# First expert's rows built by matmuls with a one-hot matrix, and each token's first expert row added by accumulating gathers at the end

## What is computed

```python
h2 = rms_norm(x, norm2_g[layer]) * (1 + sc2) + sh2
tokens = h2.reshape(b * n, d)
...
gates = jnp.sum(jax.nn.one_hot(idx, N_EXPERTS, dtype=F32) * wsel[..., None], axis=1)
for e in range(N_EXPERTS):
    he = jax.nn.silu(h @ w1[e]) * (h @ w3[e])
    y = y + gates[:, e:e + 1] * (he @ w2[e]).astype(F32)
...
x = x + g2 * f[:b * n].reshape(b, n, d)
return rms_norm(x, final_g)
```

## Time and profile before

| what | value |
|---|---|
| median of 3 runs | 601.15 us (600.04 to 601.83) |
| the profiled execution, its own time | 599.58 us |
| its span | 597.8 us |
| PE busy | 553.1 us (93%) |
| DVE busy | 442.8 us (74%) |
| ACT busy | 320.3 us (54%) |
| POOL busy | 155.7 us (26%) |
| HBM over the span | 294 GB/s |

### The profile page before, as it was taken

One profiled execution on the slowest core, in us unless ns is written; L12 is line 12 of the kernel. 1 busy time (PEld: TensorE's weight loads), 2 busy tenths in 40 slices (PEclk: granted clock), 3 DMA queues, 4 the chain that ended last, 5 costly groups with the idle time before them and its releaser, 6 DMA issues.

```text
span 597.8 us, 7516 instructions
## 1 busy us (share of the span) xinstructions
PE 553.1 (93%) x2681; PEld 412.6 (69%) x2681; DVE 442.8 (74%) x569; ACT 320.3 (54%) x394; POOL 155.7 (26%) x139
## 2 busy tenths in 40 slices
PE   1789998999999999985998999999999999999995
PEld 1345873677676787752577887888888888778772
DVE  1358693545586545428769999999999999999868
ACT  4530133345424922235438766768766768766624
POOL 5000916333220700023243113333112333110060
PEclk9789999999999999987999999999999999999998
DMA  8999997369223720058769999999999999999665
GB/s 309 389 371 321 379 369 254 101 191 357 72 70 128 247 84 36 35 210 303 241 227 390 365 398 391 392 392 392 389 392 391 390 392 390 370 383 369 209 213 210
DMA packets 89323, 172.05 MB, mean 288 GB/s; under 512 B 5514, under 2 KB 19022, under 8 KB 89298
## 3 DMA queue, kind: packets, MB, share of 16 engines
q1 hardware_dynamic: 83010, 153.34, 71.7%
q10 hardware_dynamic: 2768, 9.97, 4.1%
q0 software_dynamic: 3520, 8.42, 4.0%
HBM read 158.58 MB, written 17.32 MB: 294 GB/s over the span
## 4 chain that ended last, share of the span: by engine, by line
PE 76%; DMA 10%; DVE 5%; SPq 4%; ACT 3%; issue 1%; DVEq 0%; ACTq 0%; POOLq 0%
DMA ada<-in_ada_w 9%; PE psum L1209 5%; PE psum L1210 5%; PE psum L1211 5%; PE psum L1221 5%; PE psum L1220 5%; PE psum L1219 5%; PE psum L1236 4%; PE psum L1238 4%; PE psum L1237 4%; PE psum L934 3%; PE psum L936 3%; PE psum L935 3%; PE psum L1071 2%; PE psum L1183 2%; PE psum L1073 2%
## 5 line engine op out<-in xcount | busy, mean ns | idle before, releaser
L2116 DVE TENSOR_TENSOR w_lo<-w,w_hi 128x2048 fp32r<-128x2048 f32 x32 | 72.9, 2280 | 2.4 <-ACT w_hi L1622 2.4
L2105 DVE TENSOR_TENSOR w_lo<-w,w_hi 128x1024 fp32r<-128x1024 f32 (+2 forms) x30 | 68.7, 2293 | 0.0
L1622 ACT CAST w_hi<-w 128x2048 fp32r<-128x2048 f32 x32 | 60.3, 1918 | 10.7 <-DMA w<-in_moe_w 5.2
L1613 ACT CAST w_hi<-w 128x2048 fp32r<-128x2048 f32 x30 | 57.2, 1910 | 14.8 <-PE psum L1221 10.9
L2099 DVE TENSOR_TENSOR w_lo<-w,w_hi_a 128x2048 fp32r<-128x2048 f32 (+1 forms) x30 | 51.5, 1755 | 3.0 <-ACT w_hi_a L1609 2.7
L763 POOL COPY idx<-idx 128x1 int32 (+1 forms) x14 | 11.7, 833 | 153.0 <-PE psum L1183 152.4
L1236 PE MATMUL psum<-w_hi,heT_hi 128*128 128x512 f32 x120 | 49.7, 414 | 0.7 <-DVE w_lo L2116 0.7
L1238 PE MATMUL psum<-w_hi,heT_lo 128*128 128x512 f32 x120 | 47.0, 392 | 0.0
L1210 PE MATMUL psum<-w_lo,xgT_hi 128*128 128x512 f32 x120 | 46.8, 390 | 0.0
L1237 PE MATMUL psum<-w_lo,heT_hi 128*128 128x512 f32 x120 | 46.7, 389 | 0.0
L1219 PE MATMUL psum<-w_hi,xgT_hi 128*128 128x512 f32 x120 | 46.7, 389 | 0.0
(11 more groups left out here) (345 smaller groups left out, 1255.0 us busy)
## 6 DMA issues: line engine op xcount, KB each, us to landing
w<-in_moe_w SPq DMA_DIRECT2D x32, 2048.0 KB, 14.3
w<-in_moe_w SPq DMA_DIRECT2D x32, 1024.0 KB, 14.0
ada<-in_ada_w SPq DMA_DIRECT2D x12, 2048.0 KB, 18.1
win<-in_w_in SPq DMA_DIRECT2D x8, 1024.0 KB, 14.1
expert_rows<-ysb ACTq DMA_DIRECT2D x15, 512.0 KB, 6.3
expert_rows<-zero SPq DMA_DIRECT2D x1, 5120.0 KB, 21.3
wout<-in_w_out SPq DMA_DIRECT2D x4, 1024.0 KB, 4.9
x<-in_x SPq DMA_DIRECT2D x2, 1024.0 KB, 9.9
```

The lines of the kernel that those rows point to most:

```text
L1622: act.copy(w2_hi[:, :, hs], w2_sb[b][:, :, hs]).then_inc(w2_hi_ok[half], 1)
L2105: v.tensor_tensor(w3_lo[b][:, ks, :], w3_sb[b][:, ks, :], w3_hi[:, ks, :], ALU.subtract).then_inc(w3_lo_ok, n)
L2116: v.tensor_tensor(w2_lo[b][:, :, hs], w2_sb[b][:, :, hs], w2_hi[:, :, hs], ALU.subtract).then_inc(w2_lo_ok[half], 1)
```

## The change

The first expert's rows are no longer gathered. DVE compares slot numbers with the rank of expert 0 and multiplies by the token's choice and its norm factor (`hot_0`), PE multiplies `x1` with it, tile by tile (`first_rows`, eight feature chunks of four matmuls each), and ACT applies the norm's scale and shift of the feature (`norm_cols`) on the way to `xgT_0`. That buffer moves to the place of `xg[0]`, so that POOL clears and first uses `xg[0]` only after `plain3`. The two `keep_busy(WARM)` go, and the one ahead of the ranks gives three matmuls. At the end POOL adds each token's first row directly to `x1` by an accumulating indirect DMA; `add_first` and half of `gathered_row` go, and ACT's copy of tile 3 comes after the first tile's square.

```diff
@@ -153,6 +152,9 @@
         sq = at("sq", 196 * K1, [P, 512])
+        norm_cols = at("norm_cols", 195.125 * K1, [P, 2 * KD])
+        first_rank = at("first_rank", 195.625 * K1, [P, NT])
+        first_scale = at("first_scale", 195.75 * K1, [P, NT])
         rwq = at("rwq", 198 * K1, [P, KD, QC])
@@ -163,7 +165,8 @@
         ysb = [at(f"ysb_{b}", (176 + 4 * b) * K1, [P, D]) for b in range(2)]
-        xgT_0 = at("xgT_0", 180 * K1, [P, KD, P])
+        xgT_0 = at("xgT_0", 160 * K1, [P, KD, P])
+        hot_0 = at("hot_0", 184 * K1, [P, NT, P])
         hot_mod = at("hot_mod", 176 * K1, [P, NT * 2, P])
@@ -576,7 +579,7 @@
             load_first_w2(0)
-            sp.wait_ge(xg_in[0], 16)
+            sp.wait_ge(xg_in[1], 16)
             load_first(moe_w3, w3_sb, 1, w3_in)
@@ -746,7 +749,6 @@
             gp.wait_ge(logit_ok, NT + 1)
-            gp.memset(xg[0][:], 0.0)
             link(gp.memset(xg[1][:], 0.0))
@@ -765,8 +767,7 @@
-            for b in range(2):
-                gather_rows(b, idx[:, b:b + 1])
+            gather_rows(1, idx[:, 1:2])
@@ -784,6 +785,9 @@
             n_pairs = gp.value_load(ints[0:1, 8:9], min_val=0, max_val=OVER // 2) + NE // 2
+            gp.wait_ge(h3_ok, 1)
+            gp.sem_inc(gather_go, 1)
+            link(gp.memset(xg[0][:], 0.0))
             for b in range(2):
@@ -802,10 +806,12 @@
             for t in range(NT):
-                for k in range(2):
-                    gp.indirect_dma_start(ygat[:, t, k, :], None, y_dram,
-                                          bass.IndirectOffsetOnAxis(ap=slot_idx[:, t, k:k + 1], axis=0)
-                                          ).then_inc(gat_in[t], 16)
+                gp.indirect_dma_start(x1[:, t, :], None, y_dram,
+                                      bass.IndirectOffsetOnAxis(ap=slot_idx[:, t, 0:1], axis=0),
+                                      compute_op=ALU.add).then_inc(gat_in[t], 16)
+                gp.indirect_dma_start(ygat[:, t, 1, :], None, y_dram,
+                                      bass.IndirectOffsetOnAxis(ap=slot_idx[:, t, 1:2], axis=0)
+                                      ).then_inc(gat_in[t], 16)
@@ -1141,7 +1147,7 @@
-            keep_busy(1)
+            keep_busy(3)
             pe.wait_ge(prob_ok, 1)
@@ -1153,6 +1159,19 @@
+            def first_rows(k):
+
+                if k >= 4:
+                    pe.wait_ge(x0_ok, k - 3)
+                for t in range(NT):
+                    m = pe.matmul(bank[(0, 1, 4, 5)[k % 4]][:, 0:P], x1[:, t, k * P:(k + 1) * P], hot_0[:, t, :],
+                                  start=(t == 0), stop=(t == NT - 1))
+                m.then_inc(x0_ps, 1)
+
+            pe.wait_ge(rows_act, 8)
+            pe.wait_ge(hot0_ok, 1)
+            for k in range(4):
+                first_rows(k)
             pe.wait_ge(hot_ok, 1)
@@ -1168,26 +1187,23 @@
-            keep_busy(WARM)
-            pe.wait_ge(w1_lo_ok, 2)
-            keep_busy(WARM)
-            pe.wait_ge(rows_act, 8)
+            for k in range(4, KD):
+                first_rows(k)
...
-                pe.wait_ge(xg_in[b], i * 16 + 16)
-                if not (isinstance(s, int) and s == 0):
-                    pe.wait_ge(x_lo_ok, s)
+                pe.wait_ge(xg_in[b], (i + b) * 16)
+                pe.wait_ge(x_lo_ok, s)
                 for k in range(KD):
...
-                pe.wait_ge(x_lo_ok, 1)
                 pe.wait_ge(w1_in[0], 16)
                 for k in range(KD):
+                    pe.wait_ge(x0_ok, k + 1)
                     m = pe.matmul(bank[2][:], xgT_0[:, k, :], w1_sb[0][:, k, :], start=(k == 0), stop=(k == KD - 1))
@@ -1262,7 +1278,6 @@
-            rows_in(0, 0, 0)
             plain1()
@@ -1335,20 +1350,17 @@
             last_to_tokens(0, 1).then_inc(tok_ok, 1)
-            pe.wait_ge(x3_ok, 1)
-            for half in range(2):
-                last_to_tokens(3, half)
             pe.wait_ge(xsum_ok, 2)
...
             last_to_tokens(1, 1).then_inc(tok_ok, 1)
-            pe.wait_ge(gat_in[3], 32)
-            for half in range(2):
-                gathered_row(half, 0)
             pe.wait_ge(xsum_ok, 3)
...
             last_to_tokens(2, 1).then_inc(tok_ok, 1)
-            gathered_row(0, 1)
-            gathered_row(1, 1).then_inc(tok_ok, 1)
+            pe.wait_ge(last_act_ok, 3)
+            for half in range(2):
+                last_to_tokens(3, half)
+            gathered_row(0)
+            gathered_row(1).then_inc(tok_ok, 1)
@@ -1661,11 +1673,15 @@
             high_w1(1, 1, 0)
+            act.wait_ge(rwq_ok, 1)
+            for k in range(KD):
+                act.wait_ge(x0_ps, k + 1)
+                act.activation(xgT_0[:, k, :], bank[(0, 1, 4, 5)[k % 4]][:, 0:P], ACT.Identity,
+                               scale=norm_cols[:, k:k + 1], bias=norm_cols[:, KD + k:KD + k + 1]).then_inc(x0_ok, 1)
+            act.sem_inc(x_lo_ok, 1)
+            act.sem_inc(xt_ok, 1)
             high_w2(0, 0, 0, 0)
             high_w2(0, 0, 0, 1)
-            act.wait_ge(xt_ok, 1)
-            act.copy(xgT_0[:].rearrange("p k t -> p (k t)"), psum[:, 0:2, :].rearrange("p a n -> p (a n)")
-                     ).then_inc(x_lo_ok, 1)
             gate_half(0)
@@ -1700,17 +1716,19 @@
                 act.wait_ge((y0_copied, y1_copied)[half], last + 1)
-                act.copy(y_hi[:, hs], ysb[1][:, hs]).then_inc(ylast_hi_ok, 1)
-            act.wait_ge(fresh_ok, 4)
-            act.copy(psum[:, 6:8, :].rearrange("p a n -> p (a n)"), x1[:, 3, :]).then_inc(x3_ok, 1)
+                act.copy(y_hi[:, hs], ysb[1][:, hs]).then_inc(last_act_ok, 1)
...
                 act.activation(ygat[:, t, 0, :], psum[:, 2 * t:2 * t + 2, :].rearrange("p a n -> p (a n)"), ACT.Square,
-                               accum_out=st2[:, t, 6:7]).then_inc(ss3_ok, 1)
-                act.wait_ge(ss3_ok, t + 1)
+                               accum_out=st2[:, t, 6:7]).then_inc(ss2_ok, 1)
+                act.wait_ge(ss2_ok, 2 * NT + t + 1)
                 act.activation(st2[:, t, 7:8], st2[:, t, 6:7], ACT.Sqrt, bias=eps[:], scale=1.0 / D
-                               ).then_inc(root3_ok, 1)
+                               ).then_inc(root2_ok, 1)
+                if t == 0:
+                    act.wait_ge(gat_in[3], 32)
+                    act.wait_ge(fresh_ok, 4)
+                    act.copy(psum[:, 6:8, :].rearrange("p a n -> p (a n)"), x1[:, 3, :]).then_inc(last_act_ok, 1)
@@ -1959,6 +1977,7 @@
                 link(v.tensor_tensor(rwq[:], rw[:], bank[7][:, 128:136].unsqueeze(2).to_broadcast([P, KD, QC]), ALU.mult))
+                v.tensor_copy(norm_cols[:], bank[7][:, 128:144])
                 v.tensor_copy(shc[:], bank[7][:, 136:144].unsqueeze(2).to_broadcast([P, KD, 2])).then_inc(rwq_ok, 1)
@@ -2035,6 +2054,13 @@
             v.wait_ge(rank_ok, 1)
+            v.wait_ge(sel_ok, 1)
+            v.tensor_tensor(first_scale[:], sel[:, :, 0], st2[:, :, 4], ALU.mult)
+            link(v.tensor_copy(first_rank[:], bank[7][:, 0:NT * NE].rearrange("p (t e) -> p t e", e=NE)[:, :, 0]))
+            for t in range(NT):
+                ins = v.tensor_scalar(hot_0[:, t, :], iota_slot[:], first_rank[:, t:t + 1], first_scale[:, t:t + 1],
+                                      ALU.is_equal, ALU.mult)
+            ins.then_inc(hot0_ok, 1)
             pick(rank[:], bank[7][:, 0:NT * NE].rearrange("p (t e) -> p t e", e=NE).unsqueeze(2).to_broadcast(E2))
@@ -2202,22 +2228,19 @@
-            def add_first(t):
+            def add_second(t):
                 v.wait_ge(gat_in[t], 32)
-                link(v.tensor_tensor(x1[:, t, :], ygat[:, t, 0, :], x1[:, t, :], ALU.add))
-
-            def add_second(t):
                 v.wait_ge(fresh_ok, t + 1)
...
                 hs = slice(half * 512, (half + 1) * 512)
-                v.wait_ge(ylast_hi_ok, half + 1)
+                v.wait_ge(last_act_ok, half + 1)
                 v.tensor_tensor(y_lo[:, hs], ysb[1][:, hs], y_hi[:, hs], ALU.subtract).then_inc(ylast_lo_ok, 1)
...
             def result(t):
-                v.wait_ge(root3_ok, t + 1)
+                v.wait_ge(root2_ok, NT + t + 1)
                 link(v.reciprocal(st2[:, t, 5:6], st2[:, t, 7:8]))
@@ -2243,14 +2266,12 @@
             low_hidden(1, last)
-            add_first(0)
             expert_rows(1, last, final, 0)
...
             for t in (1, 2):
-                add_first(t)
                 add_second(t)
```

More of the change, by code:

```diff
@@ L67 @@
 K1 = 1024
-WARM = 2
 NC = N // 2 + 1
@@ L397, in build @@
         x_lo_ok = sem("x_lo_ok")
+        x0_ok = sem("x0_ok")
+        x0_ps = sem("x0_ps")
+        hot0_ok = sem("hot0_ok")
         w1_hi_ok = sem("w1_hi_ok")
@@ L411, in build @@
         xsum_ok = sem("xsum_ok")
-        x3_ok = sem("x3_ok")
         fresh_ok = sem("fresh_ok")
-        ylast_hi_ok = sem("ylast_hi_ok")
+        last_act_ok = sem("last_act_ok")
         ylast_lo_ok = sem("ylast_lo_ok")
         tok_ok = sem("tok_ok")
-        ss3_ok = sem("ss3_ok")
-        root3_ok = sem("root3_ok")
```

(6 more changed lines are left out.)

## The result

The changed kernel is slower: 605.56 us median (603.12 to 607.28) against 601.58 (600.04 to 604.01) of the kernel before, ratio 1.007 [1.0055 to 1.0084]. The forecast was 600.3; rival 2 (605.4, or 602.9 with rival 1's start) comes nearest. The profiled execution has a span of 603.4 us, 5.6 more than before, where the medians differ by 4.0: the profiled execution of the kernel before (599.58) is faster than each of its twelve timed ones (600.04 the lowest).

What follows compares the result with a forecast made beforehand. It took PE to bound the blocks, which keep their length; start +1.1 and end -1.95 gave -0.85 us on the median of 601.15, so 600.3, range 597.7 to 605.5 (the forecast's own 599 to 602).

Steps and rivals of the forecast that it cites:

- rival 2: End, ACT's wait ahead of tile 3's copy: accumulating gathers take twice as long, end +3.1, total 605.4; chance 0.32.
- rival 1: Start: the full clock holds from the first rows on, start -1.4, together -3.35, total 597.8; chance 0.25.
- both bounds: End, DMA engines' time per accumulating gather: at least a plain one's 1.48 us, at most 2.96.
- the slack I gave it: End, ACT's wait for tile 3's gathers: 0.85 us of later landing was taken to cost nothing.
- 5.9 - 0.85: End, accumulating gathers twice as long: 5.9 us more transfer time, less 0.85 of slack ahead of ACT's copy.
- the saving by the three additions and the round of `gathered_row`: End, DVE's additions and PE's gathered rows: last square starts at 590.3 instead of 592.25, -1.95 us.
- the same two changes of clock: Start: PE's clock falls at 273.7 and rises at 280.5, so index sums end at 281.9, 5.15 us later.
- the second term: Start, DVE's list behind the index sums: it can start 4.05 us later before PE's first output is late.
- The two gaps: Start, DVE's waits for PE in that list: 3.01 us ahead of 294.76 and 1.04 ahead of 302.53.
- the forecast's number: Start: index sums 5.15 later less 4.05 from DVE's gaps leave PE's first output +1.1 us.

Runs made afterwards that it cites:

- e5: The changed kernel with 25 spare matmuls on PE behind the records of tiles 0, 1 and 2 at the end; 603.67 us, ratio 1.0045 to the kernel before.
- e3: The changed kernel with its four accumulating gathers made plain, into a buffer nobody reads; 597.65 us, ratio 0.9932 to the kernel before.
- e1: The changed kernel's new start with the end of the kernel before; 600.07 us, ratio 0.9974 to the kernel before.
- e7: e1 with POOL instead of DVE adding tile 2's first gathered row to `x1`, plain gathers; 603.76 us, ratio 1.0046 to the kernel before.

## Why the prediction was wrong

**Wrong, and it set the sign:** "if an accumulating one costs what a plain one does, ACT waits for at most 0.2 us", with 1.48 taken as the likeliest value. It cost 3.0 us of the engines' time; ACT waited 5.94. I had both bounds and a stated reason for the lower one ("what is read besides lies in SBUF"), which no row supported. The upper bound was right, and rival 2's last landing (591.3 to 592) was met at 592.1. POOL's issue was also priced as a plain one's, 0.94, and took 1.55: the last gather went out at 582.72 instead of 580.13. In the changed kernel the full engines hide that. The Trainium skill's rule that I cited beside it ("Collectives: The Full Stack", Part 3: two source reads, half the rate, ratio 1.93) agrees with the ratio of 3.0 / 1.48 = 2.0 here. That a second read is the reason, no run here shows.

**Missing in every case:** what a long wait does to PE. The end cost 5.6 us, where rival 2 gave 3.1. Of the 2.5 more, 1.7 us are PE's lower clock behind the wait (e5), and 0.6 are a landing wait without the slack I gave it: from the block's end e3's copy, which waits for its gathers by 0.3, is at 12.7 and the changed kernel's 5.7 later, where I had 5.9 - 0.85. The remaining 0.2 are the next term.

**Right:** the saving by the three additions and the round of `gathered_row`, -1.95, measured -1.7 with plain gathers (e3). Right too that the blocks keep their length (265.7 us from PE's first output to the block's end, before 265.5), that ACT's eight copies and SP's `w3` load are hidden (ACT waited 0.3 us for the load), and that the first rows' records are 0.11 apart at the full clock.

**Wrong, the other way:** "I take the same two changes of clock, at 273.7 and 280.5." In the changed kernel's profile the clock was up through the first rows, rival 1's case, and the start gave -2.0 instead of +1.1 (about -1.6 by e1's ratio). At either clock the second term was off as well: DVE's list took up not 4.05 us but 5.0 of the later index sums. That is 3.05 later for an output 2.0 sooner, 4.51 for 0.5 sooner (e1), 5.93 for 0.9 later (e7), always 5.0. The two gaps are 4.05 of it; the small operations between `idx` and `hot_more` ran in 9.7 us instead of 10.5, for a reason that was not tried; 0.2 more lie behind them. Where the lower clock did hold through most of the first rows (e7), the forecast's number was nearly met: 0.9 later for its 1.1.

So a loss mis-sized by 7.6 us at the end (5.6 for -1.95) and a start mis-sized by 3.1 the other way partly met. They leave 4.5 of the 5.3 us by which the median lay above the forecast, just outside the range. That rival 2's 605.4 is so near is luck: its start (+1.1) and its end (+3.1) were both off, and in opposite directions.

## What to carry to other kernels

An accumulating gather is no free addition: it holds the DMA engines twice as long and its issue takes POOL two thirds longer, so here it would pay only with that much slack in the queue ahead of the first reader. Price an operation that no row shows by its dearer bound unless a row speaks against it. And where a change makes TensorE wait at the end of a kernel, price the matmuls behind the wait at 1.2 GHz as well as at 2.4: the difference here was 1.7 us.
